# Attention of the first block, query block by query block, with the sixteen meta keys of all heads taken together

## The chip, the cores and the metric

The kernel runs on one core of one Trainium2 chip. The metric is the device time of that core in microseconds; the kernel before takes 3743.49 us (median of 3 runs). Engines are named as the profile names them: PE (TensorE, matmuls), PEld (its weight loads), DVE (VectorE), ACT (ScalarE), POOL (GpSimd) and SP (SyncE). Everything is kept in float32; "fp32r" is a float32 that the matmul takes in one pass, and products that must be exact are made from a high and a low fp32r part.

## What is computed

Two transformer blocks. The first has two layers over 1040 positions (16 meta tokens and 1024 tokens) and holds the attention that the change touches. For every block of 128 queries, eight heads share one key and one value head of 64 numbers; an indexer has chosen 256 keys for each query, and all the others are masked:

```python
def one_block(args):                       # 128 queries qb, all 8 heads
    ...
    _, sel = lax.top_k(score, k_top)
    valid = key_chunk[sel] <= qcb[None, :, None]
    kg = gather(k, sel)
    vg = gather(v, sel)
    logits = jnp.einsum('bqhd,bqkd->bqhk', qb, kg).astype(jnp.float32) * attn_scale
    logits = jnp.where(valid[:, :, None, :], logits, NEG_INF)
    p = jax.nn.softmax(logits, axis=-1).astype(vg.dtype)
    return jnp.einsum('bqhk,bqkd->bqhd', p, vg)
```

and then, in each layer:

```python
y_a = jnp.einsum('bte,ed->btd', attn * jax.nn.silu(gate_a), w_a)
...
return x + jnp.einsum('btd,de->bte', g_a * y_a + g_b * y_b, w_out)
```

The second block (neighbourhood attention, sliding-window attention with a sink, feed-forward) is not changed but for names of semaphores.

## The kernel before

Each layer of the first block is one long sequence of projections on PE, then the attention stage, then eight "ya" projections (w_branch_a) and eight "out" projections. Each engine runs its own instruction stream in program order, written out by hand; they meet only at semaphores.

The attention stage (`attention` on PE and on DVE, `act_attention` and `move` on ACT, lists made by `units_first`) works on **units**. A unit is one head and one query block j: it sees n = 16 + 128 (j + 1) keys (`visible(j)`), from 144 for j = 0 to 1040 for j = 7; the 16 meta queries are a ninth "block", j = -1, with 16 keys. Heads are taken in four chunks c of two heads each (hh = 0, 1), and in each chunk the blocks come in the order 7, -1, 6, 0, 5, 1, 4, 2, 3, so that long and short units alternate: 72 units in a layer. A unit goes through these steps:

- PE, L503: scores, query block (high and low part stacked in 128 rows) times keys, into PSUM buffer `big[0]`; pieces of at most 512 keys, two parts each.
- DVE, L1629: masked minimum row, scale and mask, `big[0]` to `Lb`, with the row's minimum in `negmax`.
- ACT, L835: exponential, `Lb` to `Pb`, with the row's sum.
- PE, L513: transposes of `Pb` in tiles of 128 keys into `big[1]`. As n is 16 more than a multiple of 128, every unit has one more tile that holds 16 keys.
- DVE and ACT, L855 (`move`): about half of the tiles each, `big[1]` to `PT`.
- PE, L527: values, each tile of `PT` times a tile of `V`, 64 columns wide. A float32 product is two instructions, so 9 tiles are x18.
- DVE, L1643 and L1644: reciprocal and scaling of one head's 64 columns into `Ob`.
- PE, L533: every second unit, the two heads' 128 columns are turned back; DVE, L1800: times silu(gate a), into a slot of `tm`.

On PE the order in step k is: transposes of unit k-2, scores of unit k, (turn back), values of unit k-3. Scores of unit k wait for the masked step of unit k-1, since `big[0]` is single.

When a chunk is complete, ACT (L881) writes the high part of its 1044 columns into `QS` and POOL (L1273) the low part (event `attn_lo`, chunk c). POOL also loads the gates (`silu_scratch`, two slots of `tm`, the next two when a slot comes free) and, in layer 0, issues the "bands" DMAs (L1288, `band_scratch`) that a later stage needs. After the attention, PE's first ya projection takes the four chunks of `QS` one after another, each as soon as its `attn_lo` is there; POOL, after the last `attn_lo`, issues the loads of the merge gates (`gate_a_scratch`, `gate_b_scratch`), for which DVE waits in L1807.

The lines of the profile that matter outside the attention: L480 all projections, L818 and L1273 the split of weights into high and low part, L1807 and L1810 the merge.

## Time and profile before

| | us |
|---|---|
| median of 3 runs | 3743.49 (3741.01 to 3744.5) |
| span of the profiled execution | 3742.7 |
| attention stage of layer 0, first scores to the last `attn_lo` | 681.2 to 885.0 |
| attention stage of layer 1 | 1660.9 to 1864.7 |
| PE busy, whole span | 3485.0 (93%) |
| PEld / DVE / ACT / POOL busy | 3018.9 / 1925.2 / 1285.2 / 1185.7 |

The profile is of one execution, and times in it are from the start of its span. "x18" is a count of instructions; on a timeline row, like instructions that follow each other are merged, the first number is the start, the second the time to the end of the last. For PE, the PEld row of a group tells better how long it kept the engine, since the end of a matmul includes its way through the array. "PEclk" is TensorE's granted clock as a share of 2.4 GHz: 0.50 is the lower of its two levels, 1.2 GHz.

### The profile page before, as it was taken

To read this page: it belongs to the slowest core of one execution; us is meant where nothing else is said; L and a number is where in the kernel's file an instruction comes from. 1 tells how busy PE (TensorE), PEld (TensorE's weight loads), DVE (VectorE), ACT (ScalarE), POOL (GpSimd) and SP (SyncE) were. 2 spreads that over 40 slices of the span, in tenths; PEclk is the share of its full clock that TensorE was granted. 3 is DMA by queue.
4 is the path that set the end of the run, shared out by engine and by line. 5 is a ranking of instruction groups with operands and counts; after the bars stand their busy time and mean duration, and the time that the engine had idled before them with its cause. 6 is when DMAs were issued, how large, how long until landed. Compare 5 with 4: busy or idle time off the path is not lost.

```text
span 3742.7 us, 47540 instructions
## 1 busy us (share of the span) xinstructions
PE 3485.0 (93%) x18560; PEld 3018.9 (81%) x18560; DVE 1925.2 (51%) x3588; ACT 1285.2 (34%) x2072; POOL 1185.7 (32%) x697
## 2 busy tenths in 40 slices
PE   6889999999988899999998999998989899999997
PEld 5778999888977799999885877877778588888885
DVE  4568999565265799976535055544353603000014
ACT  4543221353254422125414244434342431212123
POOL 3313642104332173310153343211154342323231
PEclk8989999899999999999999999999989899999998
DMA  5101122203311012220041411111033111111111
GB/s 136 35 17 35 52 82 93 59 13 121 126 52 29 22 36 77 88 81 7 28 152 44 172 45 44 33 34 51 32 127 118 40 51 45 51 46 48 49 46 51
DMA packets 284190, 230.73 MB, mean 62 GB/s; under 512 B 31473, under 2 KB 257408, under 8 KB 283584
## 3 DMA queue, kind: packets, MB, share of 16 engines
q1 hardware_dynamic: 253792, 116.40, 11.5%
q0 software_dynamic: 23264, 85.89, 6.6%
q10 hardware_dynamic: 6912, 25.41, 1.7%
q8 instruction: 148, 2.42, 0.3%
q14 instruction: 74, 0.61, 0.1%
HBM read 177.29 MB, written 52.36 MB: 61 GB/s over the span
## 4 chain that ended last, share of the span: by engine, by line
PE 72%; issue 8%; DVE 7%; POOL 6%; ACT 4%; DMA 1%; SPq 1%; ACTq 0%; POOLq 0%; DVEq 0%
PE big L480 55%; PE small L527 6%; PE big L513 3%; PE big L503 3%; PE big L683 2%; PE small L581 1%; POOL wsp L1273 1%; DVE X L1859 1%; DMA tm<-gate_b_scratch 1%; POOL tm L1390 1%; POOL H L1273 1%; SPq L426 1%; ACT tm L1024 1%; DVE tm L1683 1%; DVE X L1863 1%
## 5 line engine op out<-in xcount | busy, mean ns | idle before, releaser
L480 PE MATMUL big<-H,wsp 128*128 128x348 f32 (+2 forms) x9984 | 1941.9, 355 | 60.0 <-POOL H L1273 30.9
L480 PEld LDWEIGHTS big<-H,wsp 128*128 128x128 f32 (+1 forms) x9984 | 1717.4, 190 | 268.3 <-issue 35.1
L1273 POOL TENSOR_TENSOR wsp<-raw,wsp 128x1024 fp32r<-128x1024 f32 (+2 forms) x246 | 543.3, 2209 | 1680.6 <-ACT wsp L818 1669.5
L480 PE MATMUL big<-SP,wsp 128*128 128x512 f32 x1920 | 451.0, 395 | 0.0
L480 PEld LDWEIGHTS big<-SP,wsp 128*128 128x128 f32 x1920 | 359.1, 187 | 90.4 <-issue 1.7
L818 ACT ACTIVATE wsp<-raw 128x1024 fp32r<-128x1024 f32 (+2 forms) x246 | 238.0, 968 | 503.2 <-PE big L480 362.7
L1778 DVE MAX8 top<-SC 128x8 f32<-128x272 f32 (+6 forms) x448 | 374.4, 836 | 0.0
L1784 DVE MATCH_REPLACE8 SC<-top,SC 128x272 f32<-128x272 f32 (+6 forms) x448 | 371.0, 828 | 0.0
L527 PE MATMUL small<-V,PT 128*128 128x64 f32 (+2 forms) x2368 | 335.5, 282 | 0.3 <-DVE tm L1891 0.3
L527 PEld LDWEIGHTS small<-V,PT 128*128 128x128 f32 (+2 forms) x2368 | 316.7, 199 | 19.7 <-issue 2.4
L1953 DVE TENSOR_TENSOR X<-X,big 128x1024 f32<-128x1024 f32 (+1 forms) x26 | 29.6, 1138 | 476.1 <-PE big L480 476.0
L835 ACT ACTIVATE Pb<-Lb,negmax 128x384 f32<-128x384 f32 (+12 forms) x272 | 191.4, 704 | 202.0 <-DVE negmax L1629 200.9
L513 PE MATMUL big<-ident,Pb 128*128 128x128 f32 x1184 | 195.3, 293 | 25.9 <-ACT PT L855 23.0
L513 PEld LDWEIGHTS big<-ident,Pb 128*128 128x128 f32 x1184 | 137.7, 149 | 49.3 <-ACT Pb L835 18.8
L855 ACT ACTIVATE PT<-big 128x256 f32<-128x256 f32 (+5 forms) x416 | 121.6, 328 | 115.9 <-PE big L513 115.1
L855 DVE COPY PT<-big 128x128 f32<-128x128 f32 (+3 forms) x256 | 108.2, 423 | 86.9 <-PE big L513 82.7
L683 PE MATMUL big<-KK,QIPB 128*128 128x512 f32 (+4 forms) x416 | 109.3, 408 | 42.2 <-ACT tm L1024 34.5
L1763 DVE SCALAR_TENSOR_TENSOR SC<-tm,widx,SC 128x272 f32<-128x272 f32 (+6 forms) x98 | 105.7, 1105 | 65.6 <-ACT tm L1024 65.3
L683 PEld LDWEIGHTS big<-KK,QIPB 128*128 128x128 f32 x416 | 82.2, 231 | 68.8 <-ACT tm L1024 50.4
L1273 POOL TENSOR_TENSOR QS<-tm,QS 128x1044 fp32r<-128x1044 f32 x8 | 19.4, 2424 | 366.7 <-ACT QS L881 366.7
L1629 DVE CUSTOM_DVE_ANT_0 Lb<-big,SC 128x1040 f32<-128x1040 f32 (+6 forms) x112 | 93.9, 838 | 64.9 <-PE big L503 64.9
L503 PE MATMUL big<-KK,QS 128*128 128x512 f32 (+4 forms) x480 | 115.9, 354 | 5.6 <-DVE negmax L1629 3.0
(205 smaller groups left out, 3361.2 us busy)
## 6 DMA issues: line engine op xcount, KB each, us to landing
raw<-in_w_in SPq DMA_DIRECT2D x108, 512.0 KB, 3.9
raw<-in_w_ff SPq DMA_DIRECT2D x64, 512.0 KB, 4.1
raw<-in_w_out SPq DMA_DIRECT2D x24, 512.0 KB, 5.3
gate_b_scratch<-tm POOLq DMA_DIRECT2D x16, 522.0 KB, 3.2
gate_a_scratch<-tm ACTq DMA_DIRECT2D x16, 522.0 KB, 2.8
tm<-gate_a_scratch POOLq DMA_DIRECT2D x16, 522.0 KB, 3.8
tm<-gate_b_scratch POOLq DMA_DIRECT2D x16, 522.0 KB, 4.6
tm<-xT_scratch POOLq DMA_DIRECT2D x16, 522.0 KB, 5.0
```

The source lines that it names most:

```text
L480: mm = pe.matmul(dst(o, width), w[wp][:, k, 0:cols], rhs(xp, k)[:, t0:t0 + width], start=(k == 0 and i == 0), stop=(k == rows - 1 and i == 2))
L503: mm = pe.matmul(big[0][:, o:o + w], u["q"], k, start=(part == 0), stop=(part == 1))
L513: mm = pe.transpose(big[1][:, at:at + P], Pb[:, u["i"] % 2, kt * P:(kt + 1) * P], ident[:])
L527: mm = pe.matmul(small[u["hh"]][:, 0:HD], PT[0:rows, u["i"] % 2, kt, :], v, start=(i == 0), stop=(i == len(u["kts"]) - 1))
L683: mm = pe.matmul(big[s][:, o:o + w], QIPB[:, 2 * (c % 2) + hh, META + j * P:META + (j + 1) * P], KK[:, part, o:o + w], start=(part == 0), ...
L818: act.activation(view(wsp[:, n % 2, 0, :]), view(raw[:, n % RAW, :]), ACT.Copy)\
L835: act.activation(Pb[:, i % 2, 0:u["n"]], Lb[:, i % 2, 0:u["n"]], ACT.Exp, bias=negmax[:, i % 4:i % 4 + 1], scale=-1.0, accum_out=rowsum[:, ...
L855: ins = eng.activation(dst, src, ACT.Copy) if who == "act" else eng.tensor_copy(dst, src)
L1273: pool.tensor_tensor(dst, src, hi.bitcast(F32), ALU.subtract).then_inc(*S.inc(name, *key))
L1763: ins = dve.scalar_tensor_tensor(sc, r, w, sc, ALU.mult, ALU.add)
L1778: dve.max(top8[:, j, :], SC[:, SCORE_AT[j]:SCORE_AT[j] + visible(j)])\
L1784: dve.match_replace(sc, top8[:, j, :], sc, TAKEN).then_inc(*S.inc("taken", l, r, j))
```

## The change

- **Order.** The units of a layer are now `for j in 7..0: for h in 0..7`, 64 of them: all eight heads of a query block one after another, all of one size. The eight meta-query units become one unit at the very end (`meta_q`: 16 queries of 8 heads are 128 rows).
- **Keys.** The tiles that are turned and multiplied start after the meta keys, so a unit has j + 1 full tiles and no tile of 16. The 16 meta probabilities of each unit are copied by POOL into `meta_p` (8 heads x 16 = 128 columns); once a block, PE turns `meta_p` and multiplies it, one product 512 columns wide, with `meta_v`, a block-diagonal copy of the meta values.
- **Output.** Eight heads share one bank of 512 columns in `small`; DVE takes one reciprocal of 8 and one scaling of 512 columns a block, PE turns four tiles back into the third bank of `big[0]`, DVE gates 512 columns at once, and ACT and POOL split each block's 512 columns into `QS` at once (`attn_hi`, `attn_lo` by block).
- **In place.** The masked row, its exponential and the transposes' source are one buffer, `rows_a`. For j = 7 the last 16 of the 1040 logits are in the third bank of `big[0]`, and DVE makes two instructions of the masked step.
- **Around it.** `tm` has no output slots any more: the four gates are loaded before the attention, ahead of the bands. The first ya projection waits for the last block's `attn_lo` before its first instruction.
- `V` is turned with the meta values in a ninth tile (one more ACT copy of 128 columns), one reduction and two small DVE instructions prepare `own_group`, `meta_q` and `meta_v`. Other edits only rename events.

```diff
+            for j in range(NQ - 1, -1, -1):
+                for h in range(HEADS):
+                    n = visible(j)
...
+                def scores(k):
+                    u = units[k]
+                    if k:
+                        pe.wait_ge(*S.at("masked", *units[k - 1]["key"]))
...
+                def turn_meta(j):
+                    pe.wait_ge(*S.at("meta_kept", "a", l, j, HEADS - 1))
...
+                    pe.transpose(big[1][:, 2 * BANK:2 * BANK + P], meta_p[:, slot_a(j), :], ident[:])\
...
+                def values_meta(j):
+                    pe.wait_ge(*S.at("meta_moved", l, j))
+                    pe.wait_ge(*S.at("meta_values", l))
+                    pe.matmul(bank_a(j)[:, :], meta_pt[:, slot_a(j), :], meta_v[:, :], start=False, stop=True,
...
-                            (lambda k: ("attn_lo", l, k)) if m == 0 else None)
+                            (lambda k: ("attn_lo", l, -1)) if m == 0 else None)
...
+                for k in range(len(units) + 8):
+                    if k < len(units):
+                        u = units[k]
+                        pool.wait_ge(*S.at("exped", *u["key"]))
...
+                        pool.tensor_copy(meta_p[:, slot_a(u["j"]), u["h"] * META:(u["h"] + 1) * META],
+                                         rows_a[:, k % 2, 0:META]).then_inc(*S.inc("meta_kept", *u["key"]))
...
+                def masked(k):
+                    u = units[k]
+                    j, h, n = u["j"], u["h"], u["n"]
+                    wait(("logits", *u["key"]))
+                    if k >= 2:
+                        wait(("turned", *units[k - 2]["key"]), ("meta_kept", *units[k - 2]["key"]))
...
+                for k in range(N + 8):
+                    if 4 <= k < N + 4 and units[k - 4]["h"] == HEADS - 1:
+                        normed_out(units[k - 4]["j"])
+                    if 2 <= k < N + 2:
+                        move_a(dve, units, k - 2, "dve")
+                    if k < N:
+                        masked(k)
+                    if k >= 7 and k - 7 < N and units[k - 7]["h"] == HEADS - 1:
+                        gated(units[k - 7]["j"])
```

POOL's queue at the start of the attention of layer 0; before:

```order
120 L1288 DMA tm<-silu_scratch 128x1044 x2
121 L1304 MEMSET zeros 2x64
122 L1288 DMA rpb_scratch<-zeros 16x1x4 x2
123 L1288 DMA rpb_scratch<-in_na_rpb 15x248
124 L1288 DMA band_scratch<-rpb_scratch 960x1x64 x8
125 L1273 TENSOR_TENSOR QS<-tm,QS 128x1044
126 L1288 DMA tm<-silu_scratch 128x1044
```

and in the changed kernel:

```order
120 L1484 DMA tm<-silu_scratch 128x1044 x4
121 L1500 MEMSET zeros 2x64
122 L1484 DMA rpb_scratch<-zeros 16x1x4 x2
123 L1484 DMA rpb_scratch<-in_na_rpb 15x248
124 L1484 DMA band_scratch<-rpb_scratch 960x1x64 x8
125 L1633 COPY meta_p<-rows_a 128x16 x16
126 L1469 TENSOR_TENSOR QS<-gated_a,QS 128x4x128
```

The loads of the third and fourth gate moved ahead of the bands, and behind the bands POOL now has a copy for every unit, which DVE's masked step of the unit after next waits for.

PE at the end of the attention of layer 0; before (L513 transposes, L503 scores, L527 values, L533 turning back, L480 the ya projections):

```order
598 L533 MATMUL small<-ident,Ob 128x128
599 L527 MATMUL small<-V,PT 128x64 x4
600 L513 MATMUL big<-ident,Pb 128x128 x5
601 L527 MATMUL small<-V,PT 128x64 x4
602 L513 MATMUL big<-ident,Pb 128x128 x5
603 L533 MATMUL small<-ident,Ob 128x128
604 L527 MATMUL small<-V,PT 128x64 x10
605 L533 MATMUL small<-ident,Ob 128x128
606 L480 MATMUL big<-QS,wsp 128x348 x288
```

and in the changed kernel (L628 and L695 transposes, L636 the turned meta keys, L691 scores, L649 and L698 values, L656 the meta values, L664 turning back, L512 the ya projections):

```order
565 L628 MATMUL big<-ident,rows_a 128x128
566 L636 MATMUL big<-ident,meta_p 128x128
567 L649 MATMUL small<-V,PT_a 128x64 x2
568 L656 MATMUL small<-meta_v,meta_pt 128x512
569 L664 MATMUL big<-ident,Ob_a 128x128 x4
570 L691 MATMUL big<-KK,meta_q 128x16 x2
571 L695 MATMUL big<-ident,rows_a 128x128
572 L698 MATMUL small<-V,PT_a 128x64
573 L664 MATMUL big<-ident,Ob_a 128x128
574 L512 MATMUL big<-QS,wsp 128x348 x288
```

What stood at the end were units of five tiles; now it is the shortest block's last unit, its block step, and then the meta-query unit, each row of which needs the one before it to have gone through other engines.

## Rows read from the trace of the kernel before

**Rows 1.** The page: busy time by engine, and the chain that ended last.

```profile
PE 3485.0 (93%) x18560; PEld 3018.9 (81%) x18560; DVE 1925.2 (51%) x3588; ACT 1285.2 (34%) x2072; POOL 1185.7 (32%) x697
PE 72%; issue 8%; DVE 7%; POOL 6%; ACT 4%; DMA 1%; SPq 1%; ACTq 0%; POOLq 0%; DVEq 0%
```

**Rows 2.** Busy time by stretch: layer 0's attention, and last the whole of layer 1's.

```profile
core 0: us, PE busy (x) PEld busy (x) DVE busy (x) ACT busy (x) POOL busy (x), PEclk, DMA share, GB/s
681.20:688.90 7.70, 4.61 (x27) 3.66 (x28) 3.21 (x7) 5.35 (x10) 3.94 (x7) 1.00 0.67 243
688.90:709.40 20.50, 20.50 (x88) 18.81 (x86) 6.84 (x24) 6.26 (x18) 6.42 (x8) 0.50 0.44 98
709.40:744.90 35.50, 35.12 (x264) 32.27 (x264) 22.24 (x74) 17.36 (x51) 0.00 (x0) 1.00 0.00 1
744.90:791.57 46.67, 45.34 (x342) 41.57 (x341) 28.84 (x99) 24.00 (x70) 2.95 (x2) 1.00 0.04 13
...
1660.90:1864.70 203.80, 195.80 (x1382) 179.09 (x1383) 115.75 (x392) 98.24 (x278) 13.05 (x10) 0.95 0.05 16
```

**Rows 3.** Timeline of the weight loads in layer 0's last chunk, by size of unit.

```profile
841.08 2.29 PEld L527 LDWEIGHTS small<-V,PT 128*128 128x128 f32 x18
...
844.64 0.29 PEld L527 LDWEIGHTS small<-V,PT 16*128 16x128 f32 x2 [0.24 <-issue]
...
848.36 0.30 PEld L503 LDWEIGHTS big<-KK,QS 128*128 128x128 f32 x2
848.60 0.14 PEld L533 LDWEIGHTS small<-ident,Ob 128*128 128x128 f32 x1
...
850.73 0.20 PEld L513 LDWEIGHTS big<-ident,Pb 128*128 128x128 f32 x2
...
854.68 0.66 PEld L527 LDWEIGHTS small<-V,PT 128*128 128x128 f32 x4
855.41 0.75 PEld L513 LDWEIGHTS big<-ident,Pb 128*128 128x128 f32 x7
```

**Rows 4.** One line's instructions: the allmean matmuls, float32, 348 and 512 columns.

```profile
L581 PE MATMUL small<-norm_sums,allmean x72: 453/456/1191, 32.4 to 2036.1; 128*128 128x348 f32 x48, 128*128 128x512 f32 x24
L581 PE MATMUL small<-norm_sums_h,allmean x48: 590/592/1191, 2925.4 to 3715.1; 128*128 128x512 f32 x48
```

**Rows 5.** Timeline of PE: transposes of equal units, 384 keys, in the sliding-window attention.

```profile
2729.79 0.85 PE L513 MATMUL big<-ident,Pb 128*128 128x128 f32 x3
...
2735.44 0.85 PE L513 MATMUL big<-ident,Pb 128*128 128x128 f32 x3
...
2740.23 0.52 PE L513 MATMUL big<-ident,Pb 128*128 128x128 f32 x3 [0.73 <-issue]
...
2744.01 0.52 PE L513 MATMUL big<-ident,Pb 128*128 128x128 f32 x3 [0.89 <-ACT PT L855]
```

**Rows 6.** Groups by shape, two chunks (744 to 838): scores' weight loads, DVE's and ACT's steps.

```profile
L503 PEld LDWEIGHTS big<-KK,QS 128*128 128x128 f32 x122 | 19.2, 192 | 1.2
L1629 DVE CUSTOM_DVE_ANT_0 Lb<-big,SC 128x1040 f32<-128x1040 f32 x4 | 5.0, 1241 | 2.5 <-PE big L503 2.5
L1629 DVE CUSTOM_DVE_ANT_0 Lb<-big,mask 128x144 f32<-128x144 f32 x4 | 1.2, 297 | 0.0
L855 DVE COPY PT<-big 128x512 f32<-128x512 f32 x9 | 6.2, 689 | 5.4 <-PE big L513 5.4
L855 ACT ACTIVATE PT<-big 128x128 f32<-128x128 f32 x8 | 2.2, 277 | 5.0 <-PE big L513 5.0
L835 ACT ACTIVATE Pb<-Lb,negmax 128x144 f32<-128x144 f32 x4 | 1.6, 407 | 0.6 <-DVE negmax L1629 0.6
L835 ACT ACTIVATION_READ_ACCUMULATOR Pb<-Lb,negmax 128x1 f32 x36 | 6.7, 187 | 0.0
```

**Rows 7.** Groups of POOL by shape, whole span: its smallest copy.

```profile
L1389 POOL COPY tm<-tm 128x8 f32<-128x8 f32 x2 | 0.4, 189 | 0.3
```

**Rows 8.** Timeline, POOL at the start of layer 0's attention.

```profile
684.56 0.53 POOL L1288 DMA_DIRECT2D tm<-silu_scratch  x1 [0.58 <-DMA gate_a_scratch<-tm]
...
690.35 6.42 POOL L1288 DMA_DIRECT2D band_scratch<-rpb_scratch  x8 [3.33 <-DMA rpb_scratch<-in_na_rpb]
```

**Rows 9.** Timeline, the end of layer 0's attention and the start of ya.

```profile
879.72 0.43 PE L527 MATMUL small<-V,PT 16*128 16x64 f32 x2
...
880.82 17.43 PE L480 MATMUL big<-QS,wsp 128*128 128x348 f32 x108
...
882.57 2.43 POOL L1273 TENSOR_TENSOR QS<-tm,QS 128x1044 fp32r<-128x1044 f32 x1 [35.35 <-ACT QS L881]
...
890.20 1.25 DVE L1807 TENSOR_TENSOR tm<-big,tm 128x1044 f32<-128x1044 f32 x1 [8.82 <-DMA tm<-gate_b_scratch]
```

**Rows 10.** Busy time by stretch: end of the sliding-window attention, and the matmuls behind it.

```profile
2750.00:2754.00 4.00, 2.60 (x20) 2.10 (x18) 3.44 (x11) 2.06 (x6) 2.92 (x2) 1.00 0.01 2
2754.00:2761.00 7.00, 5.78 (x15) 4.58 (x16) 1.32 (x7) 1.06 (x1) 4.58 (x6) 0.51 0.63 227
```

354 lines of the change are left out of this document (281 added, 73 removed).

## Prediction, before the changed kernel ran

> **What bounds the kernel now.** I began with the page: PE is busy 93% of the span, and 72% of the chain that ended last is PE [rows 1]. So a stage is worth what it asks of PE, as long as PE is what it waits for. The busy time by stretch tells whether it does [rows 2]. In the steady stretch from 744.9 to 791.57 one chunk of 18 units takes 46.67 us, with PE shown busy 45.34 of them. DVE is busy 28.84 and ACT 24.00: both have air. Both layers take 203.8 us from the first scores to the last `attn_lo`. That is four chunks of 46.67 (186.7) and 17.1 more, lost at the start: pipeline filling, and 20.5 us at PEclk 0.50, where PE had been busy only 4.61 of 7.70 us before the clock fell.
>
> The weight loads of single units [rows 3] give PE's prices. Values: x18 take 2.29 us, x4 0.66, so a tile of two instructions costs 1.63 / 7 = 0.233; the 16-key unit's pair 0.29. Transposes: x7 0.75, x2 0.20, so 0.11 each. Scores of a short unit 0.30, turning back 0.14.
>
> **The change, part by part, in one layer.** *Removed from PE.* 64 value tiles of 16 keys at 0.233, 14.9 us; 8 value pairs of meta units at 0.29, 2.3; 64 transposes at 0.11 and 8 single ones at 0.14, 8.2; 8 short scores at 0.30, 2.4. Turning back, 36 x 0.14 = 5.0, becomes 8 x 4 x 0.11 + 0.14 = 3.7: 1.3 less. Together 29.1.
>
> *Added to PE.* 8 transposes of `meta_p`, 1.1. 8 products of 512 columns: a 512-column float32 matmul is 136 ns longer than one of 348 [rows 4], so 164 columns cost 0.136 us and 512 cost 0.425; two instructions, 0.85, eight times 6.8. The single meta unit, 0.7. Together 8.6. **PE net: -20.5.**
>
> *Waits that go.* By the same prices a chunk needs: value tiles 2 x (44 x 0.233 + 8 x 0.19 + 0.29) = 24.1 (0.19 is what x4 costs over two tiles), transposes 2 x (44 x 0.11 + 0.14) = 10.0, scores 9.6 (19.2 for two chunks [rows 6]), turning back 9 x 0.14 = 1.3: 45.0 of 46.67. PE therefore waits about 1.7 a chunk. In the new order the blocks 7 to 3 (five sixths of the work) keep PE longer than DVE or ACT need: a unit of j = 7 costs PE about 4 us and DVE 1.24 + 0.69 and a small second instruction [rows 6]. I take these waits as gone, **-6** (bounds -7 and 0).
>
> *Waits that come: equal short units.* Before, a short unit stood between long ones. The nearest row is the sliding-window attention, equal units of 3 tiles [rows 5]: at full clock two take 2744.01 - 2740.23 = 3.78, so 1.89 each, where PE needs 3 x 0.11 + 0.30 + 0.89 = 1.5. For the 8 units of j = 2 most of that is the block step; I charge +0.7. For j = 0, the chain masked 0.30, exponential and its read 0.60 (one unit of ACT with its move, 0.28: 0.87) [rows 6], transposes and scores, some 2.1 us with the hand-overs, carries two units at a time: 1.05 a unit against 0.7 on PE, and once a block the scaling of 512 columns (0.69, by the copy of 512 [rows 6]) stands in front of DVE's masked step. +3.2 for j = 0, +1.5 for j = 1. **+5.4** (2 to 9).
>
> *The end.* Before, 4.85 us lay between PE's last values (to 880.15) and `attn_lo` (POOL's low part ends at 885.0), and PE filled them with the first three quarters of ya, begun at 880.82 [rows 9]. Now the steps behind the last block's meta product are a single thread: scaling, turning back, gating, exponential, transpose, move, values, scaling, turning back, gating, high part, low part. Twelve steps, most of them 0.15 to 0.7, with hand-overs: 7.4 us, my estimate from such rows. PE's own work in it, 1.3, is counted above, so 6.1 come to stand where 4.85 stood: **+1.2** (0 to 4). POOL's and ACT's last parts are short, 64 columns. Sum for layer 1: -20.5 - 6 + 5.4 + 1.2 = **-20** to `attn_lo`.
>
> *POOL in layer 0.* Each unit's masked step waits for POOL's copy two units earlier. The copy is short (189 ns for 8 columns [rows 7]; I take 0.2, upper bound the 2.4 of a full-width instruction [rows 9]), but it is queued behind everything of POOL's queue: two more gate loads at 0.53, and the bands, which end at 690.35 + 6.42 = 696.8 [rows 8]. So the first copy comes at 697.8 + 0.2. The third masked step would else be at about 690; it, the fourth scores behind it on PE, and all behind those stand still for about 9.5 us. Part of this is not lost: PE is at half clock there anyway, and work that is pushed behind the clock's rise is done at full speed. 20.5 us at half clock cost 10 us; I give back 3.5. **+6** in layer 0 only (0 to 9.5).
>
> *The clock behind the attention.* PE works little in the last 9 us. The nearest rows are the end of the sliding-window attention: PE busy 2.60 of 4.00 us, then in the seven us behind it, where the matmuls start, PEclk 0.51 [rows 10]. 6.8 us of projections at 1.2 instead of 2.4 GHz cost 3.4. Ya waited mostly for the gates' loads, which POOL issues right behind `attn_lo`, then as now (DVE waited 8.82 us and got gate b 5.2 us behind `attn_lo` [rows 9]); but the first ya now starts behind `attn_lo` and not 4.2 ahead of it. Without the clock that start would cost 0.5; with it **+3.5** a layer (0 to 6).
>
> *The clock in the last blocks.* The same row lets expect a fall within j = 0: **+1.5** a layer (0 to 7). Gates loaded early, the two preparing DVE instructions (DVE waits before the first scores) and the nine value transposes: nothing; ACT's extra copy stands before PE's next projection, +0.25 a layer.
>
> The Trainium skill has a rule against this change. Its page "TensorE: Matmul & The Clock Gate", section "Part 4: PE-mode transpose", says that transposes do not count as work in the way matmuls do for the clock. By this rule a stage of short units could stay at the lower level; that is the third rival below. The trace has PE busy 20.50 of 20.50 us at PEclk 0.50 [rows 2], with transposes and narrow values among it, which agrees without proving it.
>
> **The sum.** Layer 1: -20 + 3.5 + 1.5 + 0.25 = -14.8. Layer 0: the same + 6 = -8.8. Together -23.5: from a span of 3742.7, 3719.2. The median of the runs is 0.8 above the profiled span: **3720**.
>
> **The rivals.**
>
> *The clock rises earlier at the start.* Nothing in the trace says that the 20.5 us must repeat: the first units are now all long, with 1.1 us of scores in every one, where before two 16-key units stood. Half of it gone gives 5 us in each layer back, less in layer 0 where PE waits anyhow: -8, **3712**; with it the part of the stall that is hidden shrinks, so not lower than 3700.
>
> *The mask loop binds the long blocks too.* `big[0]` is single: scores, masked step and hand-over of j = 7 take 1.1 + 1.24 + 0.3 = 2.7 of 4 us, and DVE's block step (0.16 + 0.69) and gating (0.69) stand in the same queue. If each of the 40 long units of a layer waits 0.3 us, 2 x 12 = 24: **3744**, no change. Against it: DVE is under 60% even then.
>
> *The clock stays low from a short block on (the slower case).* At half clock, equal units of 3 tiles take 2735.44 - 2729.79 = 5.65 for two, 2.83 each against 1.89 [rows 5]. If the clock falls in j = 1, that is 8 x (0.7 + 0.4), 8.8 - 1.5 a layer: 3735. If in j = 2, 8 x 0.94 more, 7.5 a layer: **3750**. If already in j = 3, where PE's need of 2.2 us would double, 15 more a layer: **3780**, slower than before. The point from which it decides is 24 us at half clock ahead of the end, in each layer. Against it: those equal units held PEclk 1.00 for ten us in the middle, being no denser than j = 2.
>
> *It doesn't do what it says.* If the 16-key tiles cost PE nothing now because it waited anyway, only the added waits remain. Against it stands PE's need of 45.0 in 46.67; I give it nothing apart.
>
> **How the numbers follow.** Forecast 3720, by itself 3708 to 3732: 0.54. Earlier rise, about 3708: 0.2. Low from j = 1 on, 3735: 0.1. Low from j = 2 on, 3750: 0.05; from j = 3 on, 3780: 0.04. Mask loop, 3744: 0.07. The range leaves out the two lowest-chance high cases and the lower tail of the second: **3700 to 3740**. A measurement of this kernel can tell about 0.2%, 7.5 us. Faster than 3736: 0.54 + 0.2 + 0.08 = 0.82. Within 7.5 us: the rest of the third, the mask loop and most of 3750, 0.11. Slower: 0.07.
>
> **What would show it.** In the profile after: layer 0 and layer 1 differ, with DVE's masked step waiting 9 us for POOL's copy behind the bands at 690 in layer 0 alone. From first scores to the last `attn_lo` some 183 us in layer 1 (185.5 with the clock in j = 0) and 190 in layer 0. In blocks 6 to 3 PE has no waits and PEclk 1.00; a unit of j = 6 takes 3.4 us, one of j = 0 about 1.3. PE is idle for most of 7 us ahead of ya, and the first us of ya are at PEclk 0.50. It would be wrong if POOL's copy took over 1 us (then every short unit waits), if the clock fell before j = 1, if layer 0's stall did not appear, or if ya's loads were no longer what sets its pace.

## The result and the profile after

The changed kernel takes **3689.07 us** (median of 4 runs, 3687.51 to 3691.02), the kernel before on the same chip 3742.25 (3736.7 to 3744.5). The ratio is 0.9855, with a 95% interval of 0.9844 to 0.9867. The profiled span fell from 3742.7 to 3686.0 us, 56.7 less. The forecast was 3720, with a range from 3700 to 3740: the sign was right, the gain more than twice as large as forecast, and the time lies below the range.

| | before | after | forecast |
|---|---|---|---|
| span of the profiled execution | 3742.7 | 3686.0 | 3719.2 |
| layer 0, first scores to the last `attn_lo` | 203.8 | 181.1 | 190 |
| layer 0, `attn_lo` to the next norm | 135.1 | 138.8 | +3.5 |
| layer 1, first scores to the last `attn_lo` | 203.8 | 161.9 | 183 |
| layer 1, `attn_lo` to the next norm | 126.4 | 130.2 | +3.5 |

The four changes add up to -22.7 + 3.7 - 41.9 + 3.8 = -57.1 us, so the rest of the program moved by 0.4 together. These are the rows of the profile after in which the stretches begin and end, first scores (PE), last `attn_lo` (POOL), and first matmul of the next norm (PE), in layer 0 and then in layer 1 (start, duration, engine, line, operation, names, shapes, count, idle before):

```profile
678.94 0.70 PE L612 MATMUL big<-KK,QS 128*128 128x512 f32 x2 [1.33 <-ACT tm L1273]
...
859.76 0.32 POOL L1469 TENSOR_TENSOR QS<-gated_a,QS 128x64 fp32r<-128x64 f32 x1 [2.37 <-ACT QS L1011]
...
998.88 1.33 PE L721 MATMUL small<-norm_sums,allmean 128*128 128x348 f32 x4
...
1641.52 0.70 PE L612 MATMUL big<-KK,QS 128*128 128x512 f32 x2 [1.29 <-issue]
...
1803.10 0.32 POOL L1469 TENSOR_TENSOR QS<-gated_a,QS 128x64 fp32r<-128x64 f32 x1 [2.64 <-ACT QS L1011]
...
1933.57 0.59 PE L721 MATMUL small<-norm_sums,allmean 128*128 128x512 f32 x1
```

The page says little of all this: PE was 93% busy before and is 93% busy now.

```profile
PE 3414.3 (93%) x18148; PEld 2959.0 (80%) x18148; DVE 1871.1 (51%) x3271; ACT 1266.6 (34%) x1946; POOL 1212.8 (33%) x835
```

The busy time by stretch says more. Layer 1's attention as a whole answers to the last line of [rows 2]. Then come its first three stretches (up to the clock's fall, at half clock, behind it), block 6, block 2, block 1, block 0, the first 5.8 us of ya, and last the first 3.9 us of ya in layer 0. A block counts here from its first scores to those of the next block, and block 0 to its last value products:

```profile
core 0: us, PE busy (x) PEld busy (x) DVE busy (x) ACT busy (x) POOL busy (x), PEclk, DMA share, GB/s
1641.50:1803.60 162.10, 151.46 (x1151) 139.13 (x1151) 89.44 (x231) 88.36 (x214) 26.37 (x79) 0.98 0.05 19
...
1641.50:1645.60 4.10, 2.37 (x11) 1.91 (x12) 1.48 (x4) 3.02 (x4) 2.59 (x4) 1.00 0.40 152
1645.60:1649.10 3.50, 3.50 (x15) 2.96 (x15) 2.17 (x5) 1.83 (x5) 1.16 (x4) 0.52 1.02 382
1649.10:1669.97 20.87, 20.20 (x161) 19.04 (x160) 12.22 (x29) 9.73 (x17) 0.99 (x5) 1.00 0.12 48
...
1669.97:1697.06 27.09, 27.09 (x217) 25.87 (x216) 15.07 (x27) 14.06 (x26) 1.58 (x8) 1.00 0.00 1
...
1759.26:1772.47 13.21, 13.21 (x105) 12.43 (x104) 8.41 (x27) 8.64 (x27) 2.82 (x9) 1.00 0.00 1
1772.47:1783.69 11.22, 10.33 (x82) 9.07 (x80) 6.94 (x27) 7.39 (x27) 2.81 (x9) 1.00 0.01 1
1783.69:1792.80 9.11, 7.84 (x56) 6.51 (x55) 4.45 (x21) 6.37 (x27) 2.80 (x9) 1.00 0.00 0
...
1803.60:1809.40 5.80, 5.80 (x20) 5.80 (x21) 0.00 (x0) 0.00 (x0) 2.12 (x4) 0.50 0.78 282
...
860.10:864.00 3.90, 3.77 (x13) 3.80 (x14) 0.00 (x0) 0.00 (x0) 2.20 (x4) 0.50 0.62 214
```

Three things are to be seen. PE has no wait in blocks 6 and 2, 0.89 us in block 1 and 1.27 in block 0. PE is busy 151.46 us where it was 195.80, 44.3 less, while the prediction took off 20.5; some 8 us of this are the clock, since the same work keeps PE busy longer at half clock. And the stretch at half clock at the start begins 4.1 us behind the first scores and lasts 3.5 us, where before it began 7.7 us behind them and lasted 20.5.

Layer 0 is 19.2 us longer than layer 1. Its stall stands where the prediction had put it. DVE's masked step waits for POOL's first copy to `meta_p`, that copy stands behind the bands, and PE waits for the masked step (three timelines: POOL, DVE, PE; then the busy time by stretch):

```profile
691.48 6.43 POOL L1484 DMA_DIRECT2D band_scratch<-rpb_scratch  x8 [5.36 <-DMA rpb_scratch<-in_na_rpb]
697.84 0.39 POOL L1633 COPY meta_p<-rows_a 128x16 f32<-128x16 f32 x2
...
698.28 0.17 DVE L1869 CUSTOM_DVE_ANT_0 rows_a<-big,SC 128x16 f32<-128x16 f32 x1 [12.35 <-POOL meta_p L1633]
...
699.85 1.22 PE L612 MATMUL big<-KK,QS 128*128 128x512 f32 x2 [11.95 <-DVE head_min L1869]
...
687.20:699.80 12.60, 0.69 (x7) 0.46 (x5) 1.49 (x5) 0.00 (x0) 6.76 (x10) 0.61 0.70 184
699.80:717.30 17.50, 17.45 (x71) 16.29 (x72) 5.71 (x14) 5.44 (x9) 0.59 (x3) 0.50 0.12 32
```

The stall is 12 us and not 9.5, since POOL waited 5.36 us for the transfer into `rpb_scratch` where [rows 8] had 3.33. Behind it 17.5 us of dense work ran at half clock.

### The profile page after: what moved, and what is told of

It reads as the page before. It is cut to its first block, busy times and chain, and to the rows that moved or that the text cites. A ratio compares the mean times of both kernels' runs of the same rounds, so it can differ in the third digit from the quotient of the medians.

```text
span 3686.0 us, 45936 instructions
## 1 busy us (share of the span) xinstructions
PE 3414.3 (93%) x18148; PEld 2959.0 (80%) x18148; DVE 1871.1 (51%) x3271; ACT 1266.6 (34%) x1946; POOL 1212.8 (33%) x835
## 3 DMA queue, kind: packets, MB, share of 16 engines
q1 hardware_dynamic: 253792, 116.40, 11.7%
## 4 chain that ended last, share of the span: by engine, by line
PE 72%; issue 7%; DVE 7%; POOL 7%; ACT 4%; DMA 2%; SPq 1%; ACTq 0%; POOLq 0%; DVEq 0%
PE big L512 54%; PE small L649 3%; PE small L559 3%; PE big L612 2%; PE big L824 2%; PE big L628 2%; POOL wsp L1469 2%; PE big L535 2%; PE small L721 1%; PE big L545 1%; DVE X L2146 1%; POOL tm L1586 1%; POOL H L1469 1%; DMA tm<-gate_b_scratch 1%; SPq L458 1%
## 5 line engine op out<-in xcount | busy, mean ns | idle before, releaser
L512 PE MATMUL big<-H,wsp 128*128 128x348 f32 (+2 forms) x9984 | 1941.1, 355 | 59.4 <-POOL H L1469 29.8
L512 PEld LDWEIGHTS big<-H,wsp 128*128 128x128 f32 (+1 forms) x9984 | 1717.0, 190 | 266.8 <-issue 34.2
L512 PE MATMUL big<-SP,wsp 128*128 128x512 f32 x1920 | 451.0, 395 | 0.0
L512 PEld LDWEIGHTS big<-SP,wsp 128*128 128x128 f32 x1920 | 359.1, 187 | 90.4 <-issue 1.7
L649 PE MATMUL small<-V,PT_a 128*128 128x64 f32 x1152 | 150.0, 277 | 0.1
L649 PEld LDWEIGHTS small<-V,PT_a 128*128 128x128 f32 x1152 | 145.2, 196 | 3.8 <-ACT PT_a L1052 0.4
L1006 ACT ACTIVATE rows_a<-rows_a,head_min 128x1040 f32<-128x1040 f32 (+8 forms) x130 | 101.6, 782 | 128.0 <-DVE head_min L1869 128.0
L559 PE MATMUL small<-V,PT 128*128 128x64 f32 (+1 forms) x928 | 128.6, 280 | 0.2 <-DVE tm L2178 0.2
L559 PEld LDWEIGHTS small<-V,PT 128*128 128x128 f32 (+1 forms) x928 | 124.6, 200 | 5.2 <-ACT PT L996 0.3
L976 ACT ACTIVATE Pb<-Lb,negmax 128x384 f32<-128x384 f32 (+3 forms) x128 | 85.6, 668 | 83.4 <-DVE negmax L1837 83.4
L1447 ACT ACTIVATE tm<-big,b_ff 128x1024 f32<-128x1024 f32 x32 | 35.7, 1116 | 223.2 <-PE big L512 223.2
L1469 POOL TENSOR_TENSOR H<-tm,H 128x1044 fp32r<-128x1044 f32 (+3 forms) x40 | 85.4, 2139 | 78.8 <-ACT H L1078 78.8
L1633 POOL COPY meta_p<-rows_a 128x16 f32<-128x16 f32 x128 | 25.3, 199 | 255.0 <-ACT rows_a L1006 255.0
```

The lines of the kernel that those rows point to most:

```text
L512: mm = pe.matmul(dst(o, width), w[wp][:, k, 0:cols], rhs(xp, k)[:, t0:t0 + width], start=(k == 0 and i == 0), stop=(k == rows - 1 and i == 2))
L559: mm = pe.matmul(small[u["hh"]][:, 0:HD], PT[0:rows, u["i"] % 2, kt, :], v, start=(i == 0), stop=(i == len(u["kts"]) - 1))
L649: mm = pe.matmul(out[:, u["h"] * HD:(u["h"] + 1) * HD], PT_a[:, k % 2, kt, :], V[:, kt, :], start=(u["h"] == 0 and kt == 0), stop=False, s ...
L976: act.activation(Pb[:, i % 2, 0:u["n"]], Lb[:, i % 2, 0:u["n"]], ACT.Exp, bias=negmax[:, i % 4:i % 4 + 1], scale=-1.0, accum_out=rowsum[:, ...
L1006: act.activation(row, row, ACT.Exp, bias=least, scale=-1.0, accum_out=total).then_inc(*S.inc("exped", *key))
L1469: pool.tensor_tensor(dst, src, hi.bitcast(F32), ALU.subtract).then_inc(*S.inc(name, *key))
```

## The experiments

The theory that came out of the comparison had three parts. A value product of 16 keys costs far more than its weight load shows. The clock at the start of the attention is not given. And layer 0's stall costs the clock as well as itself. The rival to each is the prediction's own figure.

### What a 16-key tile gives back

```diff
+kts = [x for x in u["kts"] if x[1] == P or len(u["kts"]) == 1 or u["block"][0] != "a"]
-for i, (kt, rows, v) in enumerate(u["kts"]):
+for i, (kt, rows, v) in enumerate(kts):
```

> The kernel before, with the value products of the last 16 keys left out in the 64 units a layer that have more keys (the sum of the values lacks these keys); their transposes and moves stay. The prediction's price, 0.233 us a tile from the weight loads, gives 64 x 0.233 = 14.9 us a layer, -30 us in all: 3712. The rival takes PE's own busy time in the trace of before: 72 products of 16 keys in two steady chunks keep it busy 15.5 us, 0.215 each, 0.43 a tile: 27.5 us a layer, -55 us: 3687. A third view: if it is these narrow products that kept the clock at its lower level for 20.5 us at the start of the attention, that stretch shrinks too, to some 3 or 4 us, and another 8 us a layer go: 3671.

Measured: 3688.47 us (3685.11 to 3689.78), ratio 0.9862 (0.9847 to 0.9877). This alone is as large as the whole change. By the first of the next four rows (each a steady chunk in the middle of layer 1's attention), a chunk takes 41.01 us where it took 46.67 [rows 2]. So 16 tiles gave back 5.66 us, **0.354 us a tile** at full clock (the expectations of later runs have 0.352), 22.6 a layer, 45 of the 54 us. The rest fits the clock: the stretch at half clock was 6.8 us long in layer 0 and 3.4 in layer 1, against 20.5. The prediction's 0.233 was too low. PE's own busy time, 0.43 a tile, did go (45.34 to 38.40 us, 6.94 for 16 tiles), but not all of it was gained, since PE's waits grew from 1.33 to 2.61 us a chunk.

Without the transposes of these keys too (and with the products as above):

> The kernel before, without the value products of the last 16 keys in the units with more keys, and without the transposes of those keys (the moves stay and read what stands there; the sum of the values lacks these keys). Against the kernel without the products alone (3688) it prices 64 transposes a layer. The prediction's 0.11 us from the weight loads: -14, 3674. PE's busy time in the trace of before, 27.4 us for 180 transposes, 0.152 each: -19.5, 3669.

Measured: 3686.46 us (3684.1 to 3691.9), only 2 less than without the products alone. The chunk went from 41.01 to 39.83, 0.074 us a transpose (second row). Both expectations were too high, and the row says why: PE is busy 36.78 of 39.83 us, so it now waits 3 us a chunk.

```profile
1732.27:1773.28 41.01, 38.40 (x307) 35.98 (x307) 28.26 (x99) 23.57 (x70) 2.96 (x3) 1.00 0.04 14
...
1729.89:1769.72 39.83, 36.78 (x291) 34.21 (x291) 28.09 (x99) 23.44 (x70) 2.96 (x3) 1.00 0.05 15
...
1748.43:1792.42 43.99, 43.59 (x331) 40.25 (x330) 27.95 (x89) 23.01 (x63) 2.96 (x3) 1.00 0.05 13
...
1753.44:1796.48 43.04, 41.44 (x339) 39.47 (x339) 28.47 (x99) 23.56 (x70) 2.98 (x3) 1.00 0.05 14
```

The third row is of the kernel without the units of the meta queries, the fourth of the one with wide products, both below.

### Which product is dear: pairs put into the changed kernel

There PE is what blocks 6 to 2 wait for, so an added product shows at its full price. One pair is added in each unit, behind the others:

```diff
+mm = pe.matmul(out[:, u["h"] * HD:(u["h"] + 1) * HD], PT_a[0:16, k % 2, 0, :], V[0:16, 0, :],
+               start=False, stop=False, skip_group_check=True)
 mm.then_inc(*S.inc("weighted", *u["key"]))
```

> The changed kernel, with one more pair of value products in every one of the 64 units a layer, of 16 keys, behind the others and added to the same output (which is then no longer right). In the kernel before, leaving such a pair out gave back 0.352 us in the steady chunk, where the prediction had 0.233. If 16 keys are dear in themselves: 3689 + 128 x 0.35 = 3734. If they were dear only by what stood around them: 3689 + 128 x 0.23 = 3719, as the run with 128 keys beside it.

> The changed kernel, with one more pair of value products in every one of the 64 units a layer, of 128 keys, behind the others and added to the same output (which is then no longer right). A pair of 128 keys keeps PE busy 2 x 0.12 = 0.24 us: 3689 + 128 x 0.24 = 3720 under each theory, if PE is what the stage waits for in all its blocks; 3712 if blocks 2 to 0 have PE waiting.

> The changed kernel, with one more pair of value products in every one of the 64 units a layer, of 64 keys, behind the others and added to the same output (which is then no longer right). A pair of 16 keys put 4.05 us on every block of 8 units (0.51 a pair), one of 128 keys 1.8 (0.23). If every product that uses fewer than 128 keys pays, 64 keys cost 0.5 a pair, 4 us a block, and the time is about 3750. If the price falls with the rows in use, it lies between: some 3 us a block, 3728. If only very narrow ones pay: 1.8 us, 3708.

> The changed kernel, with two more pairs of value products in every one of the 64 units a layer, both of 16 keys, one directly behind the other (the output is then no longer right). One pair put 4.05 us on a block of 8 units. If the price belongs to each product of fewer than 128 keys, the second pair costs the same: 8.1 us a block. If it is the change between products of 128 keys and of 16, there and back, the second pair costs what one of 128 keys does, 1.8: 5.9 us a block.

> The changed kernel, with one more pair of value products in every one of the 64 units a layer, of 96 keys, behind the others and added to the same output (which is then no longer right). Pairs of 16 and of 64 keys put 4.05 us on a block of 8 units, one of 128 keys 1.8. If every product that doesn't use all 128 rows pays, 96 keys cost 4.05 us a block and some 3750 in all. If the array is split in halves or quarters for 64 rows and fewer, and only that change is paid for, 96 keys cost 1.8 us a block and 3708. The Trainium skill, page TensorEngine Tiling (Array Packing), section Available Configurations, lists row tiles of 128, 64 and 32 rows, and its section Key Properties says that a change of the tiling mode drains the engine: by these two the second.

The measure is the distance between two products of meta keys, those of block 7 and of block 6, which holds the steps of 8 units (25.87 us; from scores to scores, above, block 6 has 27.09, because other steps of its neighbours fall in between). The pairs of rows below are of the changed kernel, then with a pair of 16, of 64, of 96, of 128, and with two pairs of 16, all in layer 1 at full clock:

```profile
1679.49 1.08 PE L656 MATMUL small<-meta_v,meta_pt 128*128 128x512 f32 x2
...
1705.36 1.08 PE L656 MATMUL small<-meta_v,meta_pt 128*128 128x512 f32 x2
...
1718.32 1.12 PE L658 MATMUL small<-meta_v,meta_pt 128*128 128x512 f32 x2
...
1748.24 1.13 PE L658 MATMUL small<-meta_v,meta_pt 128*128 128x512 f32 x2
...
1710.86 1.12 PE L658 MATMUL small<-meta_v,meta_pt 128*128 128x512 f32 x2
...
1740.81 1.12 PE L658 MATMUL small<-meta_v,meta_pt 128*128 128x512 f32 x2
...
1694.47 1.08 PE L658 MATMUL small<-meta_v,meta_pt 128*128 128x512 f32 x2
...
1722.15 1.08 PE L658 MATMUL small<-meta_v,meta_pt 128*128 128x512 f32 x2
...
1694.55 1.08 PE L658 MATMUL small<-meta_v,meta_pt 128*128 128x512 f32 x2
...
1722.24 1.08 PE L658 MATMUL small<-meta_v,meta_pt 128*128 128x512 f32 x2
...
1737.69 1.13 PE L659 MATMUL small<-meta_v,meta_pt 128*128 128x512 f32 x2
...
1769.37 1.13 PE L659 MATMUL small<-meta_v,meta_pt 128*128 128x512 f32 x2
```

| added to each unit | block 6, us | more than 25.87 | a unit | time of the kernel |
|---|---|---|---|---|
| a pair of 128 keys | 27.69 | 1.82 | 0.23 | 3708.03 (3706.1 to 3711.8) |
| a pair of 96 keys | 27.68 | 1.81 | 0.23 | 3711.31 (2 runs) |
| a pair of 64 keys | 29.95 | 4.08 | 0.51 | 3748.01 (3743.34 to 3755.35) |
| a pair of 16 keys | 29.92 | 4.05 | 0.51 | 3751.11 (3743.73 to 3756.17) |
| two pairs of 16 keys | 31.68 | 5.81 | 0.73 | 3784.58 (2 runs) |

A narrow pair costs 0.51 where a wide one costs 0.23. (The wide pair added 19 us in all, near the lower figure of its expectation: in blocks 2, 1 and 0 it cost only 1.11, 0.59 and 0.45 us.) The second narrow pair adds 1.76 a block, the price of wide ones. So it is not the narrow product that is dear but **the change to it and back: 0.28 us**. 96 rows don't pay it, 64 rows pay in full. These outputs are no longer the reference's; the runs only price the products. The weight loads show where the time goes, first with the pair of 16 keys, then with that of 128 (L649 the unit's values, L651 the pair, L628 the next transposes):

```profile
1699.90 1.86 PEld L649 LDWEIGHTS small<-V,PT_a 128*128 128x128 f32 x16
1701.83 0.29 PEld L651 LDWEIGHTS small<-V,PT_a 16*128 16x128 f32 x2
1702.19 0.86 PEld L628 LDWEIGHTS big<-ident,rows_a 128*128 128x128 f32 x8
...
1700.23 1.71 PEld L649 LDWEIGHTS small<-V,PT_a 128*128 128x128 f32 x14
1701.86 0.30 PEld L651 LDWEIGHTS small<-V,PT_a 128*128 128x128 f32 x2
1702.03 0.81 PEld L628 LDWEIGHTS big<-ident,rows_a 128*128 128x128 f32 x7
```

With 128 rows a weight load begins before the one ahead has ended (1701.86 against 1700.23 + 1.71 = 1701.94), and the transposes' first begins 0.17 us behind the pair's. With 16 rows there is a gap on either side: the pair begins 0.07 behind the end of the values' loads, and the transposes 0.36 behind the pair's begin. The two differences, 0.15 and 0.19, make 0.34 us in these two units, of the size of the 0.28 by blocks. The two loads themselves take 0.29 as ever. That is why their duration, which the prediction used, said nothing of the price.

The Trainium skill, page "TensorEngine Tiling (Array Packing)", lists in its section "Available Configurations" row tiles of 128, 64 and 32 rows, and its section "Key Properties" says: "Changing tiling mode (not just tile) drains the TensorE". The runs agree: 96 rows behave as 128, 64 and 16 pay, and once for a group. The page gives no price; here it was 0.28 us there and back.

In blocks 5, 4, 3 and 2 the pair of 16 keys added 4.05, 4.00, 3.92 and 3.06 us. With 4.05 for block 7 and 3.6 for blocks 1 and 0 (where the clock was full) that is 26.7 a layer, 53 in all, where the time rose by 62. The rest fits a longer stretch at half clock at the end: 24 us in layer 1, against 10 in the changed kernel. It begins in the short blocks, with PE busy all the time:

```profile
1851.30:1860.00 8.70, 8.70 (x34) 7.52 (x35) 1.23 (x5) 3.14 (x12) 1.86 (x4) 0.50 0.01 2
```

Here block 0 took 12.83 us between the products of meta keys, where it took 9.63 in layer 0 of the same trace at full clock.

### The same, seen in the kernel before

```diff
+if rows < P and len(u["kts"]) > 1 and u["block"][0] == "a":
+    rows, kt, v = P, min(kt, 7), V[:, min(kt, 7), :]
 mm = pe.matmul(small[u["hh"]][:, 0:HD], PT[0:rows, u["i"] % 2, kt, :], v, ...
```

> The kernel before, with the value product of the last 16 keys in the 64 units a layer made over 128 rows (those of another tile, so that the output is wrong), not over 16: as many products, no narrow one. If the price is the 16 rows, a steady chunk of 46.67 us loses 16 x (0.352 - 0.23) = 2.0 us at least, by the added pairs 16 x (0.51 - 0.23) = 4.5: 16 to 36 us in all, and 10 more where the clock at the start of the attention rises earlier for it: 3700 to 3728. If the 0.352 is what any last product of a unit costs there, the chunk stays at 46.67 and the time at 3742.

Measured: **3714.16 us** (3711.91 to 3716.44), ratio 0.9916 (0.9899 to 0.9932), 30 us less with as many products. The chunk took 43.04 where it had taken 46.67 (fourth row above): 3.63 / 16 = 0.23 a tile for the change, close to the 0.28 above. Against the kernel without these products (41.01) a wide one costs 2.03 / 16 = 0.13. 8 chunks x 3.63 = 29 us. In this trace layer 0's stretch at half clock was 23.9 us long and layer 1's 3.4, so layer 0's attention became 12.5 us shorter and layer 1's 21.6: 34 together, the 29 and some 5 by the clock. The span became only 28.2 shorter. Of the 6 us between, 4.0 came back between the two layers' attentions and 3.0 behind layer 1's, while the first began 1.1 earlier; by the granted clock the trace has 54.6 us at half clock in the former stretch where that of the kernel before has 47.8, and 135.6 against 132.0 in the latter, which would be 5 of these 7 us. That 29 and 30 agree so well is thus in part chance.

### The units of the meta queries

In the kernel before, the units with j = -1 are left out (`for j in (7, 6, 0, 5, 1, 4, 2, 3)`).

> The kernel before, without the 8 units a layer of the 16 meta queries (their rows of the attention are left out). By the prediction's prices a layer loses 2.4 (scores), 1.1 (transposes), 2.3 (values) and 0.6 (turning back), 6.4 us, -13 in all; with the 7 us a layer that the clock gave back when the same two units were only moved behind the first chunk: 3742 - 13 - 14 = 3715. By PE's busy time (a pair of values 0.43, of scores 0.35, a transpose 0.15, turning back 0.29 for two units) 8.6 us a layer: 3711. If PE also waits around these units, for the chain of a unit that has almost no work of its own, they cost more: under 3705, and a steady chunk comes under 44.4 us.

Measured: 3706.11 us (3705.28 to 3708.02), ratio 0.9897 (0.9882 to 0.9912). The chunk took 43.99 (third row), 2.7 less, 10.8 a layer where the prediction had 6.4. Their products of 16 keys should pay the change of 0.28 us too, which would be 2.2 of the 4.4 more; for the rest no run has a cause. 2 x 10.8 = 21.6 leave 17 us, which fits the clock: no stretch at half clock in layer 0, one of 3.4 us in layer 1.

### What keeps the clock down at the start

```diff
-for j in (7, -1, 6, 0, 5, 1, 4, 2, 3):
+for j in ((7, 6, 0, 5, 1, 4, 2, 3, -1) if c == 0 else (7, -1, 6, 0, 5, 1, 4, 2, 3)):
```

> The kernel before, with only the two units of 16 queries moved in the first chunk, from the second place to the last: 7, 6, 0, 5, 1, 4, 2, 3, meta. If these two units, during which PE has almost no work, are what keeps the clock low, the stretch of 20.5 us shrinks to 3 to 7 and the time to about 3727. If the short units of blocks 0 and 1 between the long ones are needed for it as well, the stretch stays above 12 us here and shrinks only in the kernel with all long units first. If the order has nothing to do with it: 20.5 us and 3742.

> The kernel before, with the blocks of the first of the four chunks in the order 7, 6, 5, 4, 3, 2, 1, 0, and the 16 meta queries last; nothing else is changed. In the changed kernel layer 1's stretch at half clock at the start of the attention is 3.4 us where before it was 20.5. If the order of the units does that, the stretch shrinks here alike, and 8 us a layer go: 3725, with PE busy over 0.9 of the first 20 us. If it comes from something else in the changed kernel (no products of 16 keys, the heads of a block one after the other), the stretch stays at about 20.5 us and the time at 3742; the short units together at the end of the chunk could then cost up to 3 us a layer: 3742 to 3748.

With the meta queries later: 3731.38 us, all ten runs from 3729.35 to 3734.51, where the kernel before had 19 runs from 3732.8 to 3745.87 with median 3742.59; ratio 0.9976 (0.9966 to 0.9985). The traces, first 20.5 us behind the first 7.7 of the attention: of this kernel in layers 0 and 1, then, for comparison, of the kernel before with only its bands moved, whose layer 1 is the program of before. The last two rows are that kernel's first 7.7 us of layer 1, and the 20.5 us of layer 1 in the trace of the kernel before itself:

```profile
688.20:708.70 20.50, 20.12 (x159) 18.82 (x158) 11.55 (x40) 10.08 (x29) 6.42 (x8) 1.00 0.43 99
...
1662.80:1683.30 20.50, 19.53 (x154) 18.40 (x154) 11.78 (x39) 10.58 (x30) 0.00 (x0) 1.00 0.01 2
...
1668.50:1689.00 20.50, 19.04 (x144) 17.49 (x144) 10.81 (x38) 9.25 (x28) 0.00 (x0) 1.00 0.01 2
...
1660.80:1668.50 7.70, 5.31 (x23) 4.46 (x23) 3.28 (x7) 4.63 (x7) 2.29 (x3) 0.78 0.65 243
...
1668.60:1689.10 20.50, 20.50 (x88) 18.82 (x86) 6.83 (x24) 6.24 (x18) 0.00 (x0) 0.50 0.01 2
```

The first three have PEclk 1.00 where the kernel before has 0.50 for 20.50 us with PE busy all the time. The third and fourth are what the expectations had not foreseen: layer 1 of the kernel with only its bands moved has a short stretch within its first 7.7 us (0.78 of full clock, which is 3.4 us at half) and none behind it. **The same program of a layer, with the same order of units, can have a stretch of 3.4 us or of 20.5.** It differs between executions, and the order seems to change how often. By the attention's length, 203.8 us against 196.4, the long stretch cost 7.4 us there.

With the meta queries' units in second place the long stretch is common: the median of the kernel before is 11 us above that of this one, and its times scatter over 13 us where these ten lie within 5. With them later no long one was seen. Whether the narrow products have a part in it is not shown. Without them, in the old order, the stretches were 6.8 and 3.4 us, with wide ones in their place 23.9 and 3.4, and with the narrow ones and the bands moved 3.4 in both layers.

All long units first gave 3735.31, but from 3729.55 to 3756.45, ratio 0.9992 (0.9974 to 1.001): no difference that can be told. In its trace the start is as good (3.4 us at most); three of the ten times lie above 3750. A fall of the clock in the short units at the end of the chunk would explain them, but no trace has it.

### Layer 0's stall

```diff
 for m in range(8):
     after(("ma", l, m))
+    if l == 0 and m in (2, 5):
+        bands(m)
...
-if l == 0:
-    bands()
```

`bands(2)` issues the memset and the three stores, `bands(5)` the eight band transfers; in both kernels it is the same edit.

> The changed kernel, with the bias bands of POOL's queue (a memset, three stores, eight band transfers) issued while the ma projections run, two parts of it behind the third and the sixth of them, and no longer between the gate loads and the first copy to meta_p. The prediction charged the stall at 6 us net (9.5 less 3.5 given back): 3683. The rival takes layer 1 as the measure: its attention took 162.0 us to the last attn_lo, layer 0's 181.3, with a stall of 12 us and a stretch at half clock of 27 us against 3.4. Then the stall costs itself and the clock: 19 us, 3670. If POOL's issue of the bands delays the weights' low parts for the ma projections, a part comes back there, up to 6 us.

> The kernel before, with the bias bands of POOL's queue issued while the ma projections run, as in the changed kernel with its bands early. There nothing waited for POOL at the start of the attention, so the theory expects no change: 3742 to 3744. If the bands cost something in either kernel (the transfers beside the gate loads, POOL's hold on the weights' low parts), it shows here alike: 3730 or less, or 3750. The gain of 14 to 16 us in the changed kernel is then the change's own stall only as far as it exceeds this.

The changed kernel came to **3674.70 us** (3669.39 to 3679.93), ratio 0.983 (0.9811 to 0.9848), the fastest kernel here that leaves nothing out. Its layer 0 takes 679.76 to 841.69 = 161.9 us, where it took 181.1, as much as layer 1 (162.9 here). The kernel before came to 3740.77 against 3744.64, ratio 0.9986 (0.9971 to 1.0002): no difference that can be told. So the stall is the change's own. The profiled execution puts it at **19.2 us**, the medians at 14, and the two ratios, 0.9855 and 0.983, at 9 with intervals that overlap. The prediction had 6. It can be taken apart by the rows of the changed kernel above: 12.0 us in which PE waits, and then 17.50 us of dense work at PEclk 0.50, of which half is lost, 8.7. Their sum, 20.7, is a little over the 19.2; 0.67 us of the wait is there without the bands too, at the same unit in layer 1 (first row). With the bands early the 20.5 us behind the first 7.7 are at full clock (second row):

```profile
1651.13 0.74 PE L612 MATMUL big<-KK,QS 128*128 128x512 f32 x2 [0.67 <-DVE head_min L1869]
...
687.50:708.00 20.50, 19.83 (x159) 18.66 (x158) 12.22 (x29) 9.45 (x16) 0.99 (x5) 1.00 0.11 45
```

The 17.5 us are near the high end. The seven other traces in which the changed kernel, with products added or a part left out, still has the stall show waits of PE from 9.9 to 11.7 us, and the clock stayed at half for 8 to 11 us of work behind them in six and for 19 in one. That is why the times give less than the profiled execution.

### The two additions

The product of the meta keys made 16 columns wide (`bank_a(j)[:, 0:META]`, `meta_v[:, 0:META]`), and the single unit of the meta queries left out behind the loop:

> The changed kernel, with the product of a block's meta keys 16 columns wide instead of 512 (the share of the meta keys is missing from most of the output). The prediction priced the product of 512 columns at 0.85 us, 6.8 a layer. A pair of 16 columns still costs its two weight loads, 0.38 by their mean of 0.19: 0.47 less each time, 7.5 in all: 3681. If the products of blocks 1 and 0, where PE waits anyhow, are hidden, it is 5.6: 3683. By the duration that the trace shows, 1.08 for a pair with its pipeline, up to 11: 3678.

> The changed kernel, without the single unit of the 16 meta queries behind the last block (their rows of the attention are left out). It prices the thread at the end. In layer 1 block 0's attn_lo ends at 1800.5, that of the meta queries at 1803.4: 3 us a layer if only this goes, 3683. If the earlier start of ya also shortens the stretch at half clock behind the attention (10.2 us), another 1.7 a layer: 3680. If ya is held by its gates' loads alone, which start behind the last gating, the gain is the same 3 us, but PE's waits in ya stay as they are.

The narrow product gave 3680.04 (3676.35 to 3683.71), 9 less. Its block 6 takes 25.19 (the row's start at 1698.16 less 1672.97) against 25.87: 0.68 for 496 columns. With 0.23 for a pair (that of 64 columns above, an estimate for 16) that is 0.91 for the whole product, where the prediction had 0.85. Without the meta queries: 3680.95 (3675.75 to 3684.28), 8 less, 4 a layer. By the trace 3 of these are the thread and the stretch at half clock behind the attention fell from 10.2 to 6.8 us. The scatter of both is too wide to tell more.

```profile
1672.97 0.35 PE L656 MATMUL small<-meta_v,meta_pt 128*128 128x16 f32 x2
...
1698.16 0.35 PE L656 MATMUL small<-meta_v,meta_pt 128*128 128x16 f32 x2
```

## Why the prediction was wrong in size

The steps, in the prediction's order, for one layer unless said otherwise.

- **What bounds the kernel: right.** PE is the bound, and what leaves PE leaves the time.
- **The 16-key value tiles: the step that failed first.** 0.233 us a tile, 14.9 in all; measured 0.354 in the kernel before, 22.6 in all. The 0.233 is the difference of x18 and x4 in [rows 3], divided by the seven tiles between them. Both of these units end with a tile of 16 keys, so it cancels, and 0.233 is the price of a tile of 128 keys alone. The right price stood in the same rows: x4 is one tile of 128 keys and one of 16, 0.66 - 0.233 = 0.43. The prediction saw the 0.19 by which this is more, but booked it as a cost of each unit, under the waits, and did not take it off with the tile. PE's own busy time in the trace of before says the same, 0.215 for each 16-key product against 0.126 for the others (two steady chunks):

```profile
L527 PE MATMUL small<-V,PT 128*128 128x64 f32 x290 | 36.5, 271 | 0.0
...
L527 PE MATMUL small<-V,PT 16*128 16x64 f32 x72 | 15.5, 294 | 0.0
```

- **Their transposes:** 7.0 expected, 4.7 found when they were removed behind the products. There PE waited 3 us a chunk, and in the changed kernel it doesn't wait in blocks 6 to 2, so more is likely, but no run isolates it.
- **The meta queries' units:** priced 6.4, measured 10.8. The change of row count would explain 2.2 of the 4.4 between; the rest is open.
- **The start at half clock: the second step that failed.** The sum let its 20.5 us repeat. They did not, in layer 1: 20.5 us became 3.4, worth 8.6 as half of the difference (7.4 by the one direct pair of traces, above). That is no luck of one execution: in the nine traces of the changed kernel and its variants layer 1's stretch is 3.4 us long in three and 6.8 in six. The first rival had the mechanism, with a chance of 0.2 and a worth of 5 us a layer. The two 16-key units near the start, which it named, were the right place to look (meta queries later: 8.8 and 7.8 us in the trace's two layers, 11 in the times of both). What it lacked is that the stretch varies between executions of one program. One trace of before can't show that.
- **Waits that go, -6: plausible, not measured.** Before, PE waited 1.3 us a chunk, afterwards not at all in blocks 6 to 2. The removals measured one by one (22.6 + 4.7 + 10.8 + 8.6 for the clock = 46.7) less the net additions (7.3 the product, 1.1 its transposes, 0.7 the single unit, 2.2 the short units, 1.2 the end, less 1.3 for turning back: 11.2) come to 35.5, while the layer gave 41.9. The 6.4 between the two are of this size, but they are a remainder. A part of them can be the tiles again: each took 0.43 us of PE's time with it, of which 0.08 went into waits when they were removed alone, and 64 times this is 5 us a layer.
- **Equal short units, +5.4: too high.** PE's waits in blocks 2, 1 and 0 are 0, 0.89 and 1.27 us, 2.2 together. A unit of j = 2 takes 13.21 / 8 = 1.65 and not 1.89, one of j = 0 1.14 and not 1.3. The sliding-window units of [rows 5] were a poor neighbour, which have two heads' turning back and a sink beside them.
- **The added product, 6.8: right** (0.91 a product, 7.3), as is the unit of j = 6: 27.09 / 8 = 3.39, forecast 3.4.
- **The end, 7.4 us: right.** The last product's rows end at 1794.98 + 1.08 = 1796.06, `attn_lo` at 1803.42: 7.4.
- **The clock behind the attention, +3.5: right in size, in part by luck,** 3.7 and 3.8. In layer 1 the first 5.8 us of ya are at PEclk 0.50, 3 us lost, as forecast. In layer 0 it is only the first 3.9 us, 2 lost (last two lines of the busy time above), and the cost is the same. So ya's later start, priced at 0.5, cost more there, and no run takes the two apart.
- **The clock in the last blocks, +1.5: did not come in the changed kernel.** It stayed at 1.00 through blocks 2, 1 and 0 of layer 1. Nor did the slower case's rival. But it was near: with a pair of 16 keys more in each unit the clock fell in block 0 of layer 1 (the row of 8.70 us above), and with two in block 1 of layer 0, where it stayed at half for 35 us to the end of the attention. The Trainium skill's rule that the prediction weighed (page "TensorE: Matmul & The Clock Gate", section "Part 4: PE-mode transpose", that transposes don't count for the clock as matmuls do) had no effect here: in block 0, with a transpose for every pair of value products, PEclk is 1.00.
- **POOL in layer 0, +6: place right, the third step that failed.** The stall was 12 us, not 9.5, and in place of 3.5 us given back, some 8 more were lost in the profiled execution. The argument was that work pushed behind the clock's rise runs at full speed. But the stall itself pushed the rise back: PE was idle for 12 us, and the clock stayed low for 17.5 us of dense work behind it. Of the three steps this is the one that made the forecast too fast.

For layer 1, the terms whose measure is their own: -7.7 for the tiles, -4.4 for the meta queries' units, -8.6 for the clock at the start, -3.2 for the short units and -1.5 for the clock in them make 25.4 us more gain than forecast; with +2.3 for the transposes and +0.5 for the product, 22.6. The layer gained 41.9 where 18.5 was forecast (-20 and +1.5), 23.4 more.

## What to carry to other kernels

Price a product by PE's own busy time and by the gaps around its weight load, never by the load's duration alone: between products of 128 rows, one of 64 or of 16 rows cost 0.28 us for the change there and back. When the price of a step is taken from the difference of two units, ask which parts stand in both and cancel. Group such products, or make them wide where zeros can fill the rows; in the kernel before, 128 rows for 16 were worth 30 us without a product less. When the busiest engine comes to wait for a new step of an idle one, whatever that step is queued behind becomes part of the critical path. A stall near the start of a dense stage can cost twice, once as itself and once as the clock that rises later: here 12 us became 19 in the profiled execution, 14 by the times, and moving the transfers in the queue took it back. And look at more than one execution before a clock stretch is taken as given.
